# Order of the three products of a split weight chunk in a two-layer decoder trunk

## The reference

```python
def _swiglu(x, wg, wu, wd):
    return (jax.nn.silu(x @ wg) * (x @ wu)) @ wd

def _moe(x, router, wg, wu, wd):
    logits = (x @ router).astype(jnp.float32)
    top_val, top_idx = lax.top_k(logits, TOP_K)
    top_w = jax.nn.softmax(top_val, axis=-1)
    gate = jnp.sum(jax.nn.one_hot(top_idx, N_EXPERTS, dtype=jnp.float32) * top_w[..., None], axis=-2)
    y = jnp.zeros_like(x)
    for e in range(N_EXPERTS):
        y = y + gate[..., e:e + 1].astype(x.dtype) * _swiglu(x, wg[e], wu[e], wd[e])
    return y
```

## Time and profile before

| | |
|---|---|
| median of 3 runs | 1546.59 us (1545.77 to 1547.39) |
| the profiled execution's own time | 1543.57 us |
| its span, first to last instruction | 1541.8 us |
| mean granted TensorE clock | 0.963 |
| PE busy | 1437.3 us |
| VectorE busy | 1171.2 us |
| ScalarE busy | 1009.9 us |

### The profile page before, as it was taken

The page is one execution under the profiler, slowest core; times in us unless marked ns, Lnnn a source line. Parts: engine busy times, 40 slices in busy tenths (PEclk is TensorE's granted clock), DMA queues, the critical chain, the costliest instruction groups (busy, mean ns, idle before and its releaser), DMA issues.

```text
span 1541.8 us, 20148 instructions
## 1 busy us (share of the span) xinstructions
PE 1437.3 (93%) x7038; PEld 1197.6 (78%) x7039; DVE 1171.2 (76%) x1203; ACT 1009.9 (65%) x1155; POOL 14.0 (1%) x25
## 2 busy tenths in 40 slices
PE   6977999997787999999999999999999999999995
PEld 5755999986576788788888878888888887887884
DVE  5645454454545899899899899989989989988994
ACT  5433444444533777777787787777778777778773
POOL 2000000000000000000000000000000000000000
PEclk9978899998977899999999999999999999999998
DMA  9513454453416699899899899989989999998940
GB/s 338 189 55 109 158 183 174 155 185 119 176 55 233 245 374 364 295 370 370 324 343 368 326 341 364 373 296 370 370 294 375 368 326 334 373 366 296 373 164 27
DMA packets 176932, 420.91 MB, mean 273 GB/s; under 512 B 3664, under 2 KB 7760, under 8 KB 176896
## 3 DMA queue, kind: packets, MB, share of 16 engines
q1 hardware_dynamic: 175344, 415.40, 73.9%
q0 software_dynamic: 1552, 5.02, 1.1%
HBM read 419.36 MB, written 1.05 MB: 273 GB/s over the span
## 4 chain that ended last, share of the span: by engine, by line
PE 90%; DVE 5%; ACT 2%; issue 2%; DVEq 1%; DMA 0%; ACTq 0%
PE ps L1209 24%; PE ps L1211 24%; PE ps L1210 24%; PE ps L1368 3%; PE ps L1369 3%; PE ps L1370 3%; PE ps L1460 2%; PE ps L1491 2%; PE ps L1278 1%; PE ps L1222 1%; DVE w_lo L1112 1%; DVE h L1184 1%; ACT xn L463 1%; PE ps L1240 1%; PE ps L1529 0%
## 5 line engine op out<-in xcount | busy, mean ns | idle before, releaser
L1112 DVE TENSOR_TENSOR w_lo<-ring_a,w_hi 128x1024 fp32r<-128x1024 f32 x384 | 458.1, 1223 | 38.8 <-ACT w_hi L661 29.8
L661 ACT ACTIVATE w_hi<-ring_a 128x1024 fp32r<-128x1024 f32 x384 | 399.7, 1059 | 75.5 <-PE ps L1211 74.6
L1112 DVE TENSOR_TENSOR w_lo<-ring_b,w_hi 128x1024 fp32r<-128x1024 f32 x288 | 346.5, 1224 | 33.3 <-ACT w_hi L661 26.4
L1209 PE MATMUL ps<-w_hi,xg_hi 128*128 128x512 f32 x896 | 359.2, 401 | 9.9 <-DVE w_lo L1112 9.0
L1211 PE MATMUL ps<-w_hi,xg_lo 128*128 128x512 f32 x896 | 353.9, 395 | 0.0
L1210 PE MATMUL ps<-w_lo,xg_hi 128*128 128x512 f32 x896 | 353.9, 395 | 0.0
L661 ACT ACTIVATE w_hi<-ring_b 128x1024 fp32r<-128x1024 f32 x288 | 301.4, 1058 | 58.5 <-PE ps L1211 58.5
L749 DVE TENSOR_TENSOR w_lo<-ring_a,w_hi 128x1024 fp32r<-128x1024 f32 (+2 forms) x119 | 140.5, 1193 | 134.2 <-ACT w_hi L453 134.0
L453 ACT ACTIVATE w_hi<-ring_a 128x1024 fp32r<-128x1024 f32 (+2 forms) x119 | 121.6, 1032 | 137.0 <-PE ps L1370 69.7
L1209 PEld LDWEIGHTS ps<-w_hi,xg_hi 128*128 128x128 f32 x896 | 168.8, 188 | 51.2 <-DVE w_lo L1112 12.5
L1211 PEld LDWEIGHTS ps<-w_hi,xg_lo 128*128 128x128 f32 x896 | 169.0, 189 | 39.8
(11 more groups left out here) (261 smaller groups left out, 1469.2 us busy)
## 6 DMA issues: line engine op xcount, KB each, us to landing
ring_a<-in_moe_wg SPq DMA_DIRECT2D x40, 2048.0 KB, 7.9
ring_a<-in_moe_wu SPq DMA_DIRECT2D x32, 2048.0 KB, 8.0
ring_b<-in_moe_wd SPq DMA_DIRECT2D x32, 2048.0 KB, 7.8
ring_b<-in_moe_wu SPq DMA_DIRECT2D x24, 2048.0 KB, 8.5
ring_a<-in_moe_wd SPq DMA_DIRECT2D x24, 2048.0 KB, 7.7
ring_b<-in_moe_wg SPq DMA_DIRECT2D x16, 2048.0 KB, 7.8
ring_a<-in_ffn_wg SPq DMA_DIRECT2D x5, 2048.0 KB, 8.9
ring_a<-in_ffn_wu SPq DMA_DIRECT2D x5, 2048.0 KB, 7.6
```

The lines of the kernel that those rows point to most:

```text
L661: nc.scalar.activation(w_hi[:, (Q1 + q) % NQ, 0:1024], slot(j % RING2)[:, 1024 * k:1024 * k + 1024], ACT.Copy).then_inc(hi_done, 1)
L1112: v.tensor_tensor(w_lo[:, (Q1 + q) % NQ, 0:1024], slot(j % RING2)[:, 1024 * k:1024 * k + 1024], w_hi[:, (Q1 + q) % NQ, 0:1024].bitcast(F32 ...
L1209: pe.matmul(out_, a_hi, w_hi[:, q, c0:c1], start=first, stop=False)
```

## The change

The second and the third product of `three` change places. High activations by high weights stays first; then come low activations by high weights, and last high activations by low weights. The flags that begin and end an accumulation stay with the first and the last. The hand-written dense products L1368 to L1370 are not touched.

```diff
             def three(out_, a_hi, a_lo, q, c0, c1, first, last):
 
                 pe.matmul(out_, a_hi, w_hi[:, q, c0:c1], start=first, stop=False)
-                pe.matmul(out_, a_hi, w_lo[:, q, c0:c1], start=False, stop=False)
-                return pe.matmul(out_, a_lo, w_hi[:, q, c0:c1], start=False, stop=last)
+                pe.matmul(out_, a_lo, w_hi[:, q, c0:c1], start=False, stop=False)
+                return pe.matmul(out_, a_hi, w_lo[:, q, c0:c1], start=False, stop=last)
```

## The result

The changed kernel takes 1549.51 us, median of 20 runs (1542.65 to 1551.1), the kernel before 1546.4 us, median of 20 (1540.22 to 1550.47). The ratio is 1.0021, 95% interval 1.0012 to 1.0030. The medians differ by 3.1 us, and the interval leaves out 1: there is a real, small loss. The prediction's bound of 0.2%, also 3.1 us, lies inside the interval, so whether the loss passes it is not settled. The profiled execution of the changed kernel has a span of 1548.4 us.

The account below looks back on a forecast made before the run. PE's product pace was taken to bound the kernel; count 0, waits 0, held operand 0.3 and streamed operand 0 us on the 1546.59 us median gave 1546.8 us as written, range 1541.5 to 1552.0 us.

Parts of the forecast that it names:

- The prediction's bound of 0.2%: Whole kernel: 0.2%, 3.1 us, taken as about what a measurement can tell from no change.
- What bounds the kernel: Expert products in `three`: PE sets the pace, busy 992.5 of 1000 us; only the step between products, 231.4 ns, can move.
- count: `three`: 1644 runs, 4932 products, each still one load and one product, nothing added or removed; 0 us.
- waits: Chunk waits and releases around `three`: none needed earlier or later, ScalarE's refill of `w_hi` starts at the same moment; 0 us.
- The held operand: Activation loads in `three`: loading another tile instead of the same costs 0.2 ns by 1644, 0.3 us; upper end 5.4 us.
- the slower rival: Loads in `three`: the xg difference, 3.3 ns, is a true gain of reloading the same tile; +5.4 us, 1552.0 us, chance 0.15.
- The streamed operand: Weights in `three`: `w_hi` streaming twice in a row costs and saves nothing, judged from 128-column products; 0 us.
- What stays unknown: Product steps, up to 4% uneven: one weight buffer shifting gives 6.2 us either way, bounds -23 to +9 us; none taken.
- the likeliest case: Whole kernel: nothing moves, no step hangs on the change; 1546.8 us, alone 1544.5 to 1549.0 us, chance 0.67.
- its other reading: Weight buffers: one of four falling into the 233 ns steps gives the same sign and size; +6.2 us, 1552.8 us.
- The signs named in advance: Profile after: same load counts, 188 to 189 ns loads, hT sums within 0.3 us, six-step stretches 228 or 233 ns, eight table loads.
- Routing by rounding: Expert routing: changed rounding moves a token near a tie, so a ninth item runs; 126.6 us more, 1673 us, chance 0.01.

## Why the prediction came out as it did

*What bounds the kernel, count, waits.* Right. The same 4932 products, no wait moved by more than 0.8 us (74.6 to 75.4 us, 9.0 to 8.4 us), and in the experts, where 2.6 to 3.0 of the 3.1 us lie, the loss is the pace of the products.

*The held operand.* The price taken, 0.2 ns by 1644, rested on loads being equal whatever they load. The kernel with one held tile per triple bears that out: 0.02 us an item. The xg difference of 3.3 ns, kept as the slower rival, came back with one held tile for both loads, so it is no price of another tile; that it is the late first load fits, and was not tried by itself. This rival gave a time on the right side of before, but for a reason that is refuted. The Trainium skill, "TensorE: Matmul & The Clock Gate", Part 2, step-by-step, says that separate loads let one load once and multiply repeatedly. This program doesn't do so: 7039 loads for 7038 products in both orders. If parting the pairs had a price of its own, it would be the same at every padding, and the runs show +0.33, -0.03 and -0.09 us an item.

*The streamed operand.* Taken at nothing from 128-column products. Wrong as a proof: those rows say nothing of 512-column products in buffers that begin at different places. Nor is it quite so that no 512-wide product streamed `w_hi` twice in a row before: the third product of a triple and the first of the next did, with other columns. New are the same columns twice. Streaming them three times moved an item by 0.23 us. But "twice in a row costs" is wrong too.

*What stays unknown.* This is the term that was mis-sized. The working named the mechanism, steps that differ by how streams, loads and buffers meet, priced one shift of a buffer at 6.2 us either way, and then took 0 because the differences average out. They did not quite: the measured term is 0.33 to 0.37 us an item, 2.6 to 3.0 us in all, half of that price. The chance of 0.67 for no change leant on averaging that two stretches of a few steps cannot show.

*Sum and range.* 1546.59 + 0.3 is 1546.9, not 1546.8. The measured 1549.51 us lies inside the range of 1541.5 to 1552.0 us, but 0.5 us above the band of the likeliest case, 1544.5 to 1549.0 us. Against its own 20 runs the loss is 3.1 us where 0.3 us was forecast. The nearest to what the runs show stands in the slower rival, as its other reading: one buffer of four falling into the longer steps, priced at 6.2 us. In down the third chunk did so, from 1.372 to 1.393 us for six products. The range left room for it, but it was given no weight in the forecast, and the rival's main reading, a price for another held tile, is refuted; that the forecast comes as near as 3 us is owed to how small the effect is, and its sign was open in the working.

*The signs named in advance.* The counts, the load lengths and the eight table loads came as forecast. The hT sums did not stay within 0.3 us: by line L1211 went up 0.9 us, L1209 1.0 us, L1210 went down 0.3 us. The stretches of six steps did not stay at 1.37 and 1.40 us either. Three chunk starts in a row of the changed kernel, from its timeline:

```profile
907.43 0.40 PE L1209 MATMUL ps<-w_hi,xg_hi 128*128 128x512 f32 x1
...
908.84 0.39 PE L1209 MATMUL ps<-w_hi,xg_hi 128*128 128x512 f32 x1
...
910.22 0.39 PE L1209 MATMUL ps<-w_hi,xg_hi 128*128 128x512 f32 x1
```

These are 1.41 and 1.38 us, 235 and 230 ns a step, where a hundredth of a us is 1.7 ns. By its own tests the forecast of no shift was wrong.

*Routing by rounding.* Eight table loads, so no ninth item.

## What to carry to other kernels

Where one engine sets the pace with thousands of equal instructions, a change of order that moves no wait can still shift the pace by some 0.2% because the cost of an order hangs on where the operands lie; before explaining such a result by the order, repeat both orders with the buffers placed otherwise. If the difference changes with the place, it is no rule about orders, and the place itself is the better thing to tune: here 40 unused columns in place of 24 gained 0.4%, and none at all cost 0.7% in one execution. And read small effects from a period inside the trace, here one that repeats to 0.06 us and lies where the granted clock is 1.00, not from single executions, which scattered by several us with the clock elsewhere and once had the wrong sign.

## What the runs showed of the hardware

The step of a product that streams 512 columns at the granted clock of 1.00 depends on where the buffers lie in memory: on average 233.7, 231.4 and 230.5 ns in the hT products with 0, 24 and 40 unused columns behind each streamed chunk, the same instructions otherwise. Where the streamed buffers begin multiples of 1024 columns apart, exchanging the second and third product changes nothing (127.64 and 127.61 us an item). A tile of 64 bytes placed behind them moves single hT groups by 0.3 to 0.6 us and leaves the item at 126.59 us. A load of a tile that is already held is made all the same and takes 188 ns. Effects do not add: the new order in gate and up gave +0.09 us an item, in down -0.10, in both +0.33. What in the memory or in the engine's reads makes a step longer was not found.
